# Expert gate and up weights with eight neighbouring rows per partition, tokens gathered as whole rows on 64 partitions

## The reference, cut to what matters

```python
# t: 640 tokens x 1024; 32 experts in 4 groups; w_gate, w_up: (32, 1024, 256); w_down: (32, 256, 1024)
g_top, g_idx = lax.top_k(softmax(t @ router_group), 1)        # one group per token
e_top, e_idx = lax.top_k(e_in_group, 2)                       # two experts in that group
weights = softmax(e_top) * g_top
hid = silu(einsum('td,edf->tef', t, w_gate)) * einsum('td,edf->tef', t, w_up)
y = einsum('tef,efd->td', hid * gates[:, :, None], w_down)
```

## Time and profile before

| | before |
|---|---|
| median of three runs | 660.07 us (659.71 to 664.84) |
| the profiled execution: time / span | 659.92 us / 658.1 us |
| PE / DVE / ACT / POOL busy | 83% / 29% / 23% / 27% |
| moved by DMA | 173.15 MB in 53935 packets |
| of these on queue 1 (SP) | 153.88 MB in 45680 packets |
| granted TensorE clock | 0.957 of full speed |

### The profile page before, as it was taken

The page is one execution under the profiler, slowest core; times in us unless marked ns, Lnnn a source line. Parts: engine busy times, 40 slices in busy tenths (PEclk is TensorE's granted clock), DMA queues, the critical chain, the costliest instruction groups (busy, mean ns, idle before and its releaser), DMA issues.

```text
span 658.1 us, 9133 instructions
## 1 busy us (share of the span) xinstructions
PE 544.3 (83%) x3051; PEld 297.7 (45%) x3051; DVE 188.8 (29%) x571; ACT 151.6 (23%) x374; POOL 175.6 (27%) x242
## 2 busy tenths in 40 slices
PE   0479999999988788999997889899998778897700
PEld 0235654444445455455553446465654334454400
DVE  1150222001176765144447411111111111111027
ACT  1630102001106655122223011111111111111133
POOL 1000000002422433033334533343343222221204
PEclk9999999999997999999999899999999898899965
DMA  7999207136099500442146799999999999999368
GB/s 238 405 403 397 107 1 271 49 122 262 1 264 410 223 2 1 168 165 82 65 169 246 262 346 394 409 407 412 403 397 404 389 393 397 400 413 411 142 276 218
DMA packets 53935, 173.15 MB, mean 263 GB/s; under 512 B 7740, under 2 KB 8420, under 8 KB 52976
## 3 DMA queue, kind: packets, MB, share of 16 engines
q1 hardware_dynamic: 45680, 153.88, 60.9%
q0 software_dynamic: 7184, 15.70, 7.3%
q10 hardware_dynamic: 1008, 2.75, 1.0%
HBM read 163.75 MB, written 16.68 MB: 274 GB/s over the span
## 4 chain that ended last, share of the span: by engine, by line
PE 46%; DMA 36%; DVE 7%; SPq 3%; ACT 3%; issue 3%; POOL 1%; POOLq 0%; DVEq 0%; ACTq 0%
DMA ring<-in_w_down_dram 17%; PE ps L714 11%; PE ps L611 10%; PE ps L592 5%; PE ps L513 5%; DMA w<-in_w_down_dram 5%; DMA w_6d<-in_w_down_dram 4%; PE ps L531 3%; PE ps L593 3%; DMA w_7d<-in_w_down_dram 2%; PE ps L861 2%; DMA ring<-in_w_mod_dram 2%; PE ps L691 2%; DMA ring<-in_w_up_dram 2%; SPq L424 2%
## 5 line engine op out<-in xcount | busy, mean ns | idle before, releaser
L861 PE MATMUL ps<-ring,xt 128*64 128x256 f32 x704 | 84.1, 393 | 14.6 <-DMA ring<-in_w_up_dram 9.5
L861 PEld LDWEIGHTS ps<-ring,xt 128*64 128x64 f32 x704 | 55.7, 141 | 49.2 <-DMA ring<-in_w_up_dram 15.7
L611 PE MATMUL ps<-ring,h_t 128*128 128x512 f32 x160 | 69.5, 593 | 0.0
L1354 DVE TENSOR_TENSOR hid<-act_g,ps 128x128 f32<-128x128 f32 x32 | 9.2, 288 | 196.6 <-ACT act_g L1572 196.6
L861 PE MATMUL ps<-w,xt 128*64 128x256 f32 x416 | 51.5, 401 | 10.5 <-DMA w<-in_w_up_dram 7.5
L714 PE MATMUL ps<-ring,mix_t 128*128 128x512 f32 x120 | 53.6, 596 | 0.0
L1698 POOL DMA_INDIRECT expert_results<-y_sb,idx_out x32 | 32.8, 1024 | 59.0 <-ACT y_sb L1586 49.8
L861 PEld LDWEIGHTS ps<-w,xt 128*64 128x64 f32 x416 | 33.6, 144 | 32.7 <-DMA w<-in_w_up_dram 12.2
L611 PEld LDWEIGHTS ps<-ring,h_t 128*128 128x128 f32 x160 | 30.1, 190 | 37.6 <-issue 37.6
L592 PE MATMUL ps<-ring,h_t 128*128 128x512 f32 x80 | 42.0, 607 | 2.7 <-DVE h_t L1013 2.7
L1629 POOL TENSOR_TENSOR gm_stats<-gm_stats,half_pow 128x8 f32<-128x8 f32 x5 | 9.7, 1941 | 129.4 <-DVE gm_stats L1079 129.4
(11 more groups left out here) (239 smaller groups left out, 723.9 us busy)
## 6 DMA issues: line engine op xcount, KB each, us to landing
ring<-in_w_mod_dram SPq DMA_DIRECT2D x8, 3072.0 KB, 19.6
ring<-in_w_gate_dram SPq DMA_DIRECT2D x20, 1024.0 KB
ring<-in_w_up_dram SPq DMA_DIRECT2D x20, 1024.0 KB
ring<-in_w_down_dram SPq DMA_DIRECT2D x20, 1024.0 KB
w<-in_w_gate_dram SPq DMA_DIRECT2D x12, 1024.0 KB
w<-in_w_up_dram SPq DMA_DIRECT2D x12, 1024.0 KB
y_back<-expert_results SPq DMA_DIRECT2D x5, 1024.0 KB, 8.7
ring<-in_w_in_dram SPq DMA_DIRECT2D x2, 2048.0 KB, 17.7
```

Of the source, the lines that this page charges most:

```text
L611: last = pe.matmul(ps[:, 4 + u % 4, :], h_t[:, k, i * P:(i + 1) * P], w[:, k, :], start=(k == 0), stop=(k == KC - 1))
L861: last = pe.matmul(bank[fh * SLOT:(fh + 1) * SLOT, 0:FE].rearrange("p (a f) -> p a f", a=2), x_t[:, k % 4, (k // 4) * SLOT:(k // 4 + 1) * ...
```

## The change

Three things change together. **Weights:** partition p now holds rows 8p to 8p + 7 of the 1024 rows, one contiguous piece of 8 KB in memory for the gate and one for up. **Tokens:** slot s is one partition with the whole row of 1024; `gather` uses 64 indices and reads rows of 4 KB. Buffers 0 and 1 of `xg` share the same 8 KB per partition, on partitions 0 to 63 and 64 to 127; buffer 2 and the place of the extra tile share the other. **Transposes:** a tile is turned in 8 pieces of 64 x 128 (k = 8, every eighth column, 32 bytes apart), each giving 128 x 64. `gate_up` has the same 16 products; only the choice of the 64 columns of `xt` differs. The down weights, the scatter and the order of the work stay as they are.

```diff
-        xg = sb("xg", [P, XS, 512], F32, a0)
-        xt = sb("xt", [P, 2, 4, P], F32, a0 + 6 * KB)
+        xg = sb("xg", [P, 2, D], F32, a0)
+        xt = sb("xt", [P, 2, KC, SLOT], F32, a0 + 8 * KB)
...
-        xg_x = sb("xg_x", [P, 512], F32, b0 + 40 * KB)
-        y_sb2 = sb("y_sb2", [P, 512], F32, b0 + 42 * KB)
+        y_sb2 = sb("y_sb2", [P, 2, 512], F32, b0 + 40 * KB)
...
+        def x_rows(j):
+            return slice(SLOT * (j % 2), SLOT * (j % 2 + 1))
+
+        def x_buf(j):
+            return xg[x_rows(j), j // 2, :]
...
             def load_half(e, a):
-                sp.dma_start(weights(e)[0][:, a].rearrange("p (h k) f -> p h (k f)", h=2),
-                             (w_gate, w_up)[a][0, e].rearrange("(h p k) f -> p h (k f)", h=2, p=P)
+                sp.dma_start(weights(e)[0][:, a].rearrange("p k f -> p (k f)"),
+                             (w_gate, w_up)[a][0, e].rearrange("(p k) f -> p (k f)", p=P)
                              ).then_inc(wgu_in[e % LS], 16)
...
-            def turn_x(src, bank, done):
-                columns = src.rearrange("p (q k) -> p k q", k=4)
-                for cc in range(4):
-                    last = transpose(bank[:, cc * P:(cc + 1) * P], columns[:, cc])
+            def turn_x(j, bank, done):
+                columns = x_buf(j).rearrange("p (q k) -> p k q", k=KC)
+                for k in range(KC):
+                    last = pe.matmul(bank[:, k * SLOT:(k + 1) * SLOT], columns[:, k], ident[x_rows(j), x_rows(j)],
+                                     is_transpose=True, start=True, stop=True)
                 last.then_inc(done, 1)
...
-                                         x_t[:, k % 4, (k // 4) * SLOT:(k // 4 + 1) * SLOT],
-                                         w[:, :, k, fh * P:(fh + 1) * P], start=(k == 0), stop=(k == KC - 1))
+                                         x_t[:, k], w[:, :, k, fh * P:(fh + 1) * P], start=(k == 0), stop=(k == KC - 1))
...
+            def token_index(dst, src):
+                return dve.tensor_scalar(dst, src, 1.0, float(NO_CODE), ALU.mult, ALU.add)
...
-            row_index(idx_in[:, :, 0], ps[:, 6, 0:XS]).then_inc(rows_made, 1)
-            row_index(src_row[:, 0:EXPERTS], ps[:, 6, 0:EXPERTS])
+            token_index(idx_in[:, :, 0], ps[:, 6, 0:XS]).then_inc(rows_made, 1)
+            token_index(src_row[:, 0:EXPERTS], ps[:, 6, 0:EXPERTS])
...
-                    pool.tensor_copy(idx_in[:, j, 0:1], src_row[:, e:e + 1]).then_inc(idx_cp, 1)
+                    pool.tensor_copy(idx_in[0:SLOT, j, 0:1], src_row[0:SLOT, e:e + 1]).then_inc(idx_cp, 1)
...
-                pool.indirect_dma_start(xg[:, j, :], None, h2_halves,
-                                        bass.IndirectOffsetOnAxis(ap=idx_in[:, j, 0:1], axis=0),
-                                        bounds_check=2 * TILES * P - 1, oob_is_err=False).then_inc(xg_in[j], 16)
+                pool.indirect_dma_start(x_buf(j), None, h2_dram,
+                                        bass.IndirectOffsetOnAxis(ap=idx_in[0:SLOT, j, 0:1], axis=0),
+                                        bounds_check=TILES * P - 1, oob_is_err=False).then_inc(xg_in[j], 16)
...
-            pool.memset(xg_x[:], 0.0).then_inc(xg_zero, 1)
+            pool.memset(x_buf(XS), 0.0).then_inc(xg_zero, 1)
```

More of the change, by code:

```diff
@@ L169, in hybrid_dit_step @@
         mix_t = sb("mix_t", [P, KC, TILES * P], F32, a0)
-        xg = sb("xg", [P, XS, 512], F32, a0)
-        xt = sb("xt", [P, 2, 4, P], F32, a0 + 6 * KB)
[L172 to L175, removed]
+        xg = sb("xg", [P, 2, D], F32, a0)
+        xt = sb("xt", [P, 2, KC, SLOT], F32, a0 + 8 * KB)
+        act_g = sb("act_g", [P, 2, P], F32, a0 + 12 * KB)
+        hid = sb("hid", [P, 2, P], F32, a0 + 13 * KB)
+        hid_t = sb("hid_t", [P, 2, P], F32, a0 + 14 * KB)
+        y_sb = sb("y_sb", [P, 512], F32, a0 + 15 * KB)
         act_x = sb("act_x", [P, P], F32, a0 + 17 * KB)
@@ L273, in hybrid_dit_step @@
         y_dram = nc.dram_tensor("expert_results", [TILES * P, TOPK, D], F32, kind="Internal").ap()
-        h2_halves = h2_dram.rearrange("t (h n) -> (t h) n", h=2)
         y_halves = y_dram.rearrange("t k (h n) -> (t k h) n", h=2)
@@ L359, in y_buf @@
         def y_buf(c):
-            return y_sb2[:, :] if c % XS == 2 else y_sb[:, c % XS]
+            return y_sb[:, :] if c % XS == 0 else y_sb2[:, c % XS - 1]
+        def x_rows(j):
+            return slice(SLOT * (j % 2), SLOT * (j % 2 + 1))
+        def x_buf(j):
+            return xg[x_rows(j), j // 2, :]
         def loads(c):
@@ L877, in next_x @@
                     pe.wait_ge(x_cp, e - 1)
-                turn_x(xg[:, e % XS], ps[:, e % 2, :], x_tr)
+                turn_x(e % XS, ps[:, e % 2, :], x_tr)
             def products(e):
@@ L907, in expert @@
                     pe.wait_ge(e_in, 16 * (x + 1))
-                    turn_x(xg_x[:, :], ps[:, xb, :], e_tr)
+                    pe.sem_inc(seen, 1)
+                    turn_x(XS, ps[:, xb, :], e_tr)
                     pe.wait_ge(e_cp, x + 1)
@@ L1331, in extra_rows @@
                 dve.wait_ge(r_idx, 3)
-                row_index(src_row[:, EXPERTS:], ps[:, 6, 128:128 + N_X])
+                token_index(src_row[:, EXPERTS:], ps[:, 6, 128:128 + N_X])
                 row_index(dst_row[:, EXPERTS:], ps[:, 6, 128 + N_X:128 + 2 * N_X]).then_inc(rows_made, 1)
@@ L1347, in copy_x @@
                     dve.wait_ge(gu2_mm, e - 1)
-                dve.tensor_copy(xt[:, e % 2].rearrange("p c s -> p (c s)"), ps[:, e % 2, :]).then_inc(x_cp, 1)
+                dve.tensor_copy(xt[:, e % 2].rearrange("p k s -> p (k s)"), ps[:, e % 2, :]).then_inc(x_cp, 1)
             def hidden(e):
@@ L1366, in expert @@
                     dve.wait_ge(e_tr, x + 1)
-                    dve.tensor_copy(xt[:, xb].rearrange("p c s -> p (c s)"), ps[:, xb, :]).then_inc(e_cp, 1)
+                    dve.tensor_copy(xt[:, xb].rearrange("p k s -> p (k s)"), ps[:, xb, :]).then_inc(e_cp, 1)
                     dve.wait_ge(e_silu, x + 1)
@@ L1702, in gather_extra @@
             def gather_extra(x):
-                pool.tensor_copy(idx_x[:, 0:1], src_row[:, bass.ds(EXPERTS + x, 1)]).then_inc(e_idx, 1)
+                pool.tensor_copy(idx_x[0:SLOT, 0:1], src_row[0:SLOT, bass.ds(EXPERTS + x, 1)]).then_inc(e_idx, 1)
                 pool.wait_ge(e_idx, x + 1)
                 pool.sem_inc(seen, 1)
-                pool.indirect_dma_start(xg_x[:, :], None, h2_halves,
-                                        bass.IndirectOffsetOnAxis(ap=idx_x[:, 0:1], axis=0),
-                                        bounds_check=2 * TILES * P - 1, oob_is_err=False).then_inc(e_in, 16)
+                pool.indirect_dma_start(x_buf(XS), None, h2_dram,
+                                        bass.IndirectOffsetOnAxis(ap=idx_x[0:SLOT, 0:1], axis=0),
+                                        bounds_check=TILES * P - 1, oob_is_err=False).then_inc(e_in, 16)
             def extras(e):
```

## The result

The changed kernel takes 677.48 us in the median of four runs (676.01 to 678.26), the kernel before 659.89 beside it: a ratio of 1.0246, 95% interval 1.0195 to 1.0297. It is 17.6 us slower, where 657.1 was forecast. The profiled execution has a span of 674.1 us, 16.0 more than before.

A forecast was written before the change was run, and what follows sets the result against it. The DMA engines' own time was taken to bound the stage. From 659.9 us profiled, -4.8 for loads, +0.75 ahead and +0.95 behind gave 656.8, or 657.0 against the median; 657.1 was predicted, 8-in-10 range 652.8 to 662.3.

The forecast's parts named there:

- What bounds the kernel: From 379 to 602 us the DMA engines' own time bounds the stage, not a queue or a wait; 8.69 us per expert.
- Part 1: Gate and up loads: one 8 KB piece costs 12 ns less than two of 4 KB; 4.8 us saved over 25 loads.
- Rival 2: Gate and up loads gain nothing, as pieces are cut to the same packets or memory binds: 661.8 us; chance 0.14.
- rival 1: Gate and up loads: the longer piece also removes slow stretches, bringing 8.8 us: 653.0 us; chance 0.15.
- The sign that I named: Gate loads from expert 14 to 31: a pitch of 8.5 us, 8.69 before, would show the forecast right.
- Part 2: Token turns: 8 transposes for 4 make a turn 1.22 us, 0.47 more; covered in the stage, exposed at both ends.
- Rival 3: Transposes: a 32-byte step costs twice the pitch of 16 bytes, making a turn 1.4 us longer: 660.9 us; chance 0.07.
- Part 3: Gathers: same bytes, 64 indices take POOL 0.8 us; -0.5 us ahead of the stage, landing time left at 3.5 us.
- Rival 4: Stage: gathers on 64 partitions crowd 8 of 16 DMA engines, 0.4 us more per expert: 667 us; chance 0.05.
- Part 3 and 4: Ahead of the stage: gathers -0.5 us, clearing the extra tile's place +0.5; with first turns' +0.75, +0.75 in all.

The follow-up runs named there:

- e1: The kernel before with only the gate and up loads changed to one piece of 8 KB per partition; ratio 0.9944 to the kernel before.
- e8: The kernel before with gate and up in 8 KB pieces and norm rows written in another column order, half-row gathers kept; ratio 0.9939.
- e2: The changed kernel with gate and up loads as before (4 KB pieces) and transposes taking columns 16 bytes apart; ratio 1.0261 to the kernel before.
- e9: The changed kernel with a 4 KB buffer per gather, whole rows to partitions 0 to 63 and 64 to 127 by turns; ratio 1.0228.
- e10: As e9, with all whole rows put on partitions 32 to 95; ratio 1.0002 to the kernel before, 663.6 us.
- e6: The changed kernel gathering half rows of 2 KB to partitions 0 to 63 and 64 to 127 by turns; ratio 0.9966 to the kernel before.
- e7: As e6, with every gather of half rows going to partitions 32 to 95; ratio 0.9880 to the kernel before.
- e13: The kernel before with one constant changed, spreading the used slots over groups of partitions; ratio 0.9940 to the kernel before.
- e11: As e9, with all whole rows put on partitions 0 to 63; ratio 1.0193 to the kernel before.
- e15: The changed kernel with the spread slots of e13, nothing else; ratio 1.0153 to the kernel before, 673 us.
- e17: As e10, with the used slots spread evenly over both halves and all groups of partitions; ratio 0.9913 to the kernel before.
- e18: As e12, with the used slots spread as in e13 and e15; ratio 1.0070 to the kernel before.
- e12: As e11, but the gather has 128 indices, the upper 64 out of bounds; ratio 1.0201 to the kernel before.
- e16: As e14, with down weights in 8 KB pieces too and gate_up taking every second column of the weights; ratio 0.9883 to the kernel before.
- e14: As e8, with the spread slots of e13; ratio 0.9874 to the kernel before, 655.1 us.

## Why the prediction was wrong, by its own steps

**What bounds the kernel: right.** The stage is bound by DMA, and the loss is there, about 0.54 us for each of 25 experts. (The sum of the terms is 656.8, or 657.0 against the median; the 657.1 forecast is a slip of 0.1.)

**Part 1, pieces of 8 KB: right.** Forecast 4.8 us (none to 8.8); e1 measured 0.56% (0.35 to 0.76), 3.7 us (2.3 to 5.0). The price of 310 ns per piece of 8 KB against 322 for two of 4 came from two windows of one trace and carried well. The estimate from the 3 cycles of the Trainium skill ("DMA: Bandwidth & Descriptors"), 1.4 us, is under the interval. Rival 2 is out by e1; so is rival 1, since the interval ends at 5.0. The sign that I named, a pitch of 8.5 from expert 14 to 31, didn't come: 8.69 in e1, 8.61 in e8. That stretch of one execution is too rough to tell these from each other.

**Part 2, the transposes: right in kind, a little high.** A turn is 1.03 us on the chain in place of 1.22; the stretch behind the last load grew by 0.61 and not by 0.95. Rival 3 is refuted by e2, whose load is from 64 partitions as well: with columns 32 bytes apart it takes 202 ns in the median and a turn 1.03 us, at 16 bytes apart (e2) 215 ns and 1.10 us. By the Trainium skill's lines of 16 bytes ("SBUF — State Buffer", the note on cachelines) a new line costs; the wider step is no dearer here.

**Part 3, the gathers: the step that failed.** I priced POOL's instruction and wrote "the same bytes", with the landing time left as it was and no term at all for what the gathers do to the weight loads beside them. In the stage the gathers went from what their bytes are worth to some 19 us more. What the runs show in place of the missing term: where the rows are written slows all transfers together (e9 against e10, 15 us with nothing else changed; e6 against e7). Rival 4 came nearest, and I gave it 0.05 and 0.4 us per expert, but its mechanism isn't what was found. It had half of the engines crowded and the rest waiting, with a share under 1; the share stayed at 0.99 to 1.02, and the packets stretched. Measured, the pitch rose by 0.64 with the gain of the pieces in it, and the time was 677 and not 667. The two reasons I held against it fail: that the stage has a DMA share of 1.02 says nothing, for it stays 1.02 (e9) while the packets stretch; and that 128 partitions with two halves are uneven as well is true, but e13 shows that this unevenness had its price too, 0.6%, in the kernel before. I also had the turns of the halves even out a third of it; e11 against e9 shows that they even out nothing.

The Trainium skill ("SBUF — State Buffer", Door 1: The DMA port swizzle) says that a range of partitions from 0 to 63 reaches only 8 of the 16 ports by which DMA enters that memory, that 64 to 127 reach the other 8, and that four partitions share a port with the four 32 further on. By this rule 32 to 95 reach all 16, and the traces agree for a full tile: expert 0's gather lands after 3.54 us in e10 and 4.03 in e9. For the stage it isn't shown that the rule is enough: by it an expert of up to 32 tokens has its rows on the same ports in e10 as in e11, and e10 is 1.9% faster over all. The rule also says which slots to spread, and e13, e15, e17 and e18 all gained.

**Part 3 and 4, ahead of the stage.** From the start of the first gather to expert 5's load it took 20.2 us where it took 17.7, +2.5 against a forecast of +0.75. The first gather lands after 3.98 us in place of 3.60; `products(0)` starts 2.15 us behind that in place of 1.80; it takes 5.37 for 5.25; the clearing takes 0.947 us for 0.526, about the doubling I took; and the gather of the extra tile lands after 4.79 us, not 3.50. POOL's gather instruction went only from 1.04 to 0.98 us, not to 0.8. So the landing time was the wrong one to leave alone. For the first gather that is the rows' place: 4.03 us in e9 against 3.54 in e10. For the extra tile's it isn't settled: in e1, whose gathers are as before, that landing took 5.22 us.

**What stays open.** By which rule the place of the rows sets the cost in the stage: the half, the group of eight and the sharing out over the engines each fit some of the runs, and none of them all. Why the turns of the halves even nothing out while two loads are in flight; how the rest of e15's cost divides between the half and the engines; and why e18 gained by spreading more than e15 did.

## What to carry to other kernels

When DMA bounds a stage, ask of every transfer in it onto which partitions it writes, not only how many bytes it has: 5.2 MB of gathers beside 82 MB of weights cost 32 us as whole rows on 64 partitions, and 12 as half rows on all 128. A DMA share of 1 doesn't show this; the engine time per byte of the other queue does. And where a tile is padded, spread the used slots over the partitions: in this kernel it is one constant, and with the longer pieces and the permuted rows of e8 it gives 1.26%.

## What the runs showed of the hardware that I had not expected

- Rows of 4 KB written to partitions 0 to 63 lower the rate of all DMA together from about 401 to 380 GB/s, though the share stays at 1.01 to 1.02; the same rows at 32 to 95 don't (e11 and e10), although most of the used ones still lie under 64.
- With 128 indices of which half are out of bounds the share falls under 1 (0.99) at the same rate as with 64 (1.01): engines wait a little, and 4 KB takes 169 ns of engine time in place of 172 (e12, e11). Alone, such a gather of 64 rows lands after 4.49 us in place of 4.10.
- A weight load of 128 columns from 64 partitions with a step of 32 bytes takes 202 ns, with a step of 16 bytes 215 (e2), and one of 128 columns from 128 partitions with a step of 16 bytes 209.
- POOL and ACT write pieces of 16 bytes as fast as contiguous rows, within 1% (e8: 1458 and 1280 ns for 128 x 512 on POOL and 716 on ACT, 1458, 1269 and 714 before).
- Reading every second column of the weights (8 bytes apart) makes 32 products 3.85 us long in place of 3.67 (e16, e14).
